# Modulation vectors of a diffusion backbone layer: ada weights as the stationary operand

## The reference, cut to what matters

```python
silu_c = jax.nn.silu(c)              # (1, 1024)
silu_cc = jax.nn.silu(c_ctx)         # (1024,)
sh1, sc1, gt1, sh2, sc2, gt2 = split(silu_c @ ada_w + ada_b, 6)       # ada_w (1024, 6144)
csh1, csc1, cgt1, csh2, csc2, cgt2 = split(silu_cc @ ada_w + ada_b, 6)
hc = modulate(rmsnorm(ctx, norm1_g), csh1, csc1)    # h * (1 + scale) + shift
hx = modulate(rmsnorm(x, norm1_g), sh1, sc1)
...                                  # token mixers (RWKV-7 and mLSTM), merge, gt1
...                                  # second modulation (sh2, sc2), PEER experts, gt2
```

## Time and profile before

| what | value |
|---|---|
| time, median of 3 runs | 3191.59 us (3189.38 to 3191.71) |
| profiled execution: time | 3191.34 us |
| profiled execution: span on the core | 3189.6 us |
| PE, matmul records busy | 2753.4 us (86% of the span) |
| PE, weight loads busy | 2209.1 us (69%) |
| DVE / ACT / POOL busy | 1354.8 / 1006.7 / 701.0 us |
| mean granted TensorE clock | 0.919 of full speed |

### The profile page before, as it was taken

How to read it: one execution, slowest core, us unless ns; L and a number is a source line. 1 busy time by engine, 2 the same in 40 slices (tenths; PEclk the granted TensorE clock), 3 DMA queues, 4 the chain that set the end, 5 groups by cost and what they waited for, 6 DMA issues and landing times. The chain is left out here.

```text
span 3189.6 us, 54953 instructions
## 1 busy us (share of the span) xinstructions
PE 2753.4 (86%) x20248; PEld 2209.1 (69%) x20248; DVE 1354.8 (42%) x2852; ACT 1006.7 (32%) x1666; POOL 701.0 (22%) x540
## 2 busy tenths in 40 slices
PE   5798867657748895996996999999799999999998
PEld 1684144436638883875885788888688888888886
DVE  1221214445566655222899444444001444444443
ACT  2221111141322123223321566666223222222222
POOL 0520000001011202343444555554343000000000
PEclk9899955568979998998998999999899999999999
DMA  4210500000000002222322354544543655555552
GB/s 162 80 58 30 217 0 0 0 7 1 8 1 0 0 5 104 88 86 83 119 88 83 122 207 161 199 176 161 207 148 112 235 190 188 201 190 187 200 192 79
DMA packets 159924, 349.01 MB, mean 109 GB/s; under 512 B 13224, under 2 KB 79272, under 8 KB 156528
## 3 DMA queue, kind: packets, MB, share of 16 engines
q1 hardware_dynamic: 159856, 348.10, 31.4%
HBM read 276.75 MB, written 71.30 MB: 109 GB/s over the span
## 5 line engine op out<-in xcount | busy, mean ns | idle before, releaser
L85 PE MATMUL ps_a<-h_hi,u_hi 128*128 128x512 f32 x1024 | 407.3, 398 | 23.1 <-PEq L105 16.5
L86 PE MATMUL ps_a<-h_hi,u_lo 128*128 128x512 f32 x1024 | 401.0, 392 | 0.0
L87 PE MATMUL ps_a<-h_lo,u_hi 128*128 128x512 f32 x1024 | 400.7, 391 | 0.0
L2360 DVE TENSOR_TENSOR v_lo<-v_raw,v_hi 128x1024 fp32r<-128x1024 f32 x128 | 158.2, 1236 | 564.8 <-ACT v_hi L2318 564.8
L85 PE MATMUL ps_y<-gated_hi,v_hi 128*128 128x512 f32 x768 | 299.5, 390 | 3.1 <-DVE gated_lo L2362 3.1
L86 PE MATMUL ps_y<-gated_hi,v_lo 128*128 128x512 f32 x768 | 299.5, 390 | 0.0
L87 PE MATMUL ps_y<-gated_lo,v_hi 128*128 128x512 f32 x768 | 299.3, 390 | 0.0
L2318 ACT ACTIVATE v_hi<-v_raw 128x1024 fp32r<-128x1024 f32 x128 | 135.8, 1061 | 478.4 <-PE ps_a L87 470.0
L85 PEld LDWEIGHTS ps_a<-h_hi,u_hi 128*128 128x128 f32 x1024 | 194.1, 190 | 62.2 <-issue 22.7
L87 PEld LDWEIGHTS ps_a<-h_lo,u_hi 128*128 128x128 f32 x1024 | 193.6, 189 | 41.0
L86 PEld LDWEIGHTS ps_a<-h_hi,u_lo 128*128 128x128 f32 x1024 | 193.9, 189 | 37.7
(11 more groups left out here) (478 smaller groups left out, 5595.6 us busy)
## 6 DMA issues: line engine op xcount, KB each, us to landing
u_raw<-in_uT SPq DMA_DIRECT2D x128, 512.0 KB, 3.5
v_raw<-in_v SPq DMA_DIRECT2D x128, 512.0 KB, 4.9
a_scratch<-act SPq DMA_DIRECT2D x128, 256.0 KB, 2.2
w_scratch<-w_block SPq DMA_DIRECT2D x8, 4096.0 KB, 12.0
w_ring<-w_scratch SPq DMA_DIRECT2D x64, 512.0 KB, 4.6
gated<-a_scratch SPq DMA_DIRECT2D x128, 256.0 KB, 5.0
ada_ring<-in_ada_w SPq DMA_DIRECT2D x12, 2048.0 KB, 7.9
mg_raw<-in_w_merge SPq DMA_DIRECT2D x36, 512.0 KB, 3.5
```

Of the source, the lines that this page charges most:

```text
L85: pe.matmul(out, wh, xh, start=first, stop=False)
L86: pe.matmul(out, wl, xh, start=False, stop=False)
L87: return pe.matmul(out, wh, xl, start=False, stop=last)
L2360: v.tensor_tensor(vl[:, q], v_raw[:, q], vh[:, q], ALU.subtract).then_inc(v_lo, 1)
```

## The change

The ada weights become the stationary operand and the two conditioning columns the moving one. For each tile, each group of 128 columns and each of the 8 blocks of rows there is one matmul, with 128 x 128 of the ada weights stationary and 128 x 2 of `silu_c` moving; the 8 of a group accumulate in PSUM, in the two columns of `ps_mod` where the turned row stood. `copy_row`, `turn`, the row buffers in SBUF and PSUM and their semaphores go. `add_bias` waits for the last tile's matmuls. The DMAs, the ring of two tiles and its wait stay as they are.

```diff
-    def __init__(self, nc, ctx, a, b, tag, lo, hi, row):
+    def __init__(self, nc, ctx, a, b, tag, lo, hi):
...
-        self.row = row
-        self.ps_row = [ctx.enter_context(nc.psum_tensor(f"ps_row{k}" + tag, [P, MOD_W], F32)) for k in range(2)]
...
     def multiply(self, pe, n):
         pe.wait_ge(self.ring_in[n % 2], (n // 2 + 1) * 16)
-        if n >= 2:
-
-            pe.wait_ge(self.out, n - 1)
-        for k in range(KT):
-            mm = pe.matmul(self.ps_row[n % 2][0:2, :], self.b.silu_c[:, k, :], self.ring[:, n % 2, k, :],
-                           start=(k == 0), stop=(k == KT - 1))
+        for q in range(PER):
+            o = 2 * (n * PER + q)
+            for k in range(KT):
+                mm = pe.matmul(self.ps_mod[:, o:o + 2], self.ring[:, n % 2, k, q * P:(q + 1) * P],
+                               self.b.silu_c[:, k, :], start=(k == 0), stop=(k == KT - 1))
         mm.then_inc(self.mm, 1)
-
-    def copy_row(self, act, n):
-        act.wait_ge(self.mm, n + 1)
-        act.activation(self.row[:, n, :], self.ps_row[n % 2][0:2, :], ACT.Copy).then_inc(self.out, 1)
-
-    def turn(self, pe):
-        pe.wait_ge(self.out, self.hi - self.lo)
-        for n in range(self.hi - self.lo):
-            for q in range(PER):
-                o = 2 * (n * PER + q)
-                mm = pe.matmul(self.ps_mod[:, o:o + 2], self.row[:, n, q * P:(q + 1) * P], self.b.ident[0:2, 0:2],
-                               start=True, stop=True)
-        mm.then_inc(self.turned, 1)
...
-        v.wait_ge(self.turned, 1)
+        v.wait_ge(self.mm, self.hi - self.lo)
```

More of the change, by code:

```diff
@@ L130, in __init__ @@
         self.bias = ctx.enter_context(nc.sbuf_tensor("ada_bias" + tag, [P, N_MOD * KT], F32))
-        self.row = row
-        self.ps_row = [ctx.enter_context(nc.psum_tensor(f"ps_row{k}" + tag, [P, MOD_W], F32)) for k in range(2)]
         self.ps_mod = ctx.enter_context(nc.psum_tensor("ps_mod" + tag, [P, 512], F32))
         self.ring_in = [b.semaphore(nc, f"ada_in{k}" + tag) for k in range(2)]
-        self.bias_in, self.mm, self.out, self.turned, self.done = (
-            b.semaphore(nc, f"mod_{n}" + tag) for n in ("bias_in", "mm", "row_out", "turned", "done"))
+        self.bias_in, self.mm, self.done = (b.semaphore(nc, f"mod_{n}" + tag) for n in ("bias_in", "mm", "done"))
     def load(self, sp, n):
@@ L201, in phase_modulation @@
         dve = sem("mod_dve")
-        mod = Modulation(nc, ctx, a, b, "_1", 0, MOD_FIRST, b.qX[0:2, :, :])
+        mod = Modulation(nc, ctx, a, b, "_1", 0, MOD_FIRST)
         block = ctx.enter_context(nc.Block())
@@ L233, in _ @@
             act.activation(rs[:], rs[:], ACT.Exp, scale=-0.5).then_inc(root_done, 1)
-            for n in range(MOD_FIRST):
-                mod.copy_row(act, n)
             for j in range(KT):
@@ L261, in _ @@
                 mod.multiply(pe, n)
-            mod.turn(pe)
         @block.vector
@@ L1121, in phase_mlstm_gates @@
         rows_done = sem("mlg_rows")
-        mod = Modulation(nc, ctx, a, b, "_2", MOD_FIRST, MOD_TILES, b.acc[0:2, :, :])
+        mod = Modulation(nc, ctx, a, b, "_2", MOD_FIRST, MOD_TILES)
         n_mod = MOD_TILES - MOD_FIRST
@@ L1146, in _ @@
             act.activation(bsum[:], bsum[:], ACT.Ln, bias=1.0).then_inc(act_done, 1)
-            for n in range(2):
-                mod.copy_row(act, n)
             act.wait_ge(want[1], 1)
@@ L1152, in _ @@
             act.activation(rows[:, 4], rows[:, 4], ACT.Exp).then_inc(act_done, 1)
-            for n in range(2, n_mod):
-                mod.copy_row(act, n)
         @block.vector
```

## The result

The changed kernel takes 3288.07 us (median of 4 runs, 3287.61 to 3289.9); the kernel before 3191.32 us (4 runs). The ratio is 1.0305, 95% interval 1.0288 to 1.0323: 3.1% slower, 96.8 us. The profiled execution took 3287.61 us with a span of 3285.6 us. I had forecast 3247 and a range up to 3268: the sign was right and the size too small by 41 us.

The account below looks back on a forecast made before the run. PE's modulation stream was taken to set the end of both phases, at a clock fallen to 0.50. Terms of +18.0 and +38.1 us, +56.1 on 3191.34, gave 3247 us; range 3208 to 3268 for 8 in 10.

Parts of the forecast that it names:

- Which stream sets the end, and that DMAs hide: Both modulation phases: PE's stream sets the end, each microsecond of it counts in the kernel, and all tile DMAs are hidden.
- The clock: Both modulation phases: the new stream lets PE's clock fall at 40.5 us and never raises it from 0.50.
- loads count: Rival, both modulation phases: weight loads of 128 rows hold and raise the clock; -15.1 us, 3176 us; chance 13%.
- the turning's fall at 408.1: Second phase before the change: the clock fell from 1.00 to 0.50 while PE turned, taken as evidence for the new stream.
- The pace: Modulation: a 128-column load with a 2-column matmul takes 0.109 us at 2.4 GHz and 0.2136 us at 1.2 GHz.
- Latency: Rival, modulation: each of 16 matmuls adding to the same PSUM columns may wait for the last; +162 us, 3353; chance 5%.
- the check over 63 steps: Turning in the second phase: 22 steps at one pace and 41 at the other, 11.15 us, agreed with the paces.
- The two terms: Lengthening of the modulation's PE stream: +18.0 us in the first phase and +38.1 us in the second.
- The trust in a page's load rule: Modulation loads: the page's rule gives 107 ns for 128 columns at either clock; the sum used the trace's 214 ns at 1.2 GHz.
- The program's growth: PE's program: 480 more pairs in straight code; fetching could leave gaps, but 64 turning pairs ran without one; no time added.

## Why the prediction was right and wrong

*Which stream sets the end, and that DMAs hide.* Right. DVE's adds follow PE's last pair directly; no tile's DMA but the first of the second phase is waited for.

*The clock.* Right. It fell under loads of 128 rows as under the turning's 2, and the rival "loads count" is out: in the second phase 512 pairs, each half of them without a gap, left it at 0.50. What I had leaned on, the turning's fall at 408.1, carried over.

*The pace.* Right: 0.213 us measured for 0.2136. "Latency" is out. One sum on the way is wrong: (2.42 + 0.18) / 22 is 0.118 and not 0.11. The stretch began with the first pair, so that nothing reaches in over its edge, and 2.42 / 22 = 0.11 is the right reading; the check over 63 steps gives the same, and the 0.109 used carries no error from it.

*The two terms.* 16.6 and 37.4 us, 54.0 together, for 18.0 and 38.1. In the first phase the fast stretch lasted until just before 40, some 5 us, where I allowed 3.9; the transposes took 1.4 us, not 1.9. When the clock falls differs from one execution to the next: with the loop held at slot 40 it fell some 2.4 us into the phase, and the bias add came 52.5 us after PE's start, 19.0 us more than before. PE began the first phase 2.0 us earlier in this execution, and from the first bias add to the second phase's start it took 0.9 us less; that brings the 54.0 to the 51.1 us seen at the next phase. With the loop held in place the whole kernel gave 53.6.

*The trust in a page's load rule.* I had weighed a load at its columns over 1.2 ns (the Trainium skill, "TensorE: Matmul & The Clock Gate", section LDWEIGHTS) against the trace, and had gone by the trace. The measurement keeps to that: 0.213 us a pair at the lower level.

*The program's growth.* Here the prediction failed. It said: "PE's program grows by 768 - 288 = 480 pairs in straight code; fetching it could leave gaps, but 64 pairs of turning ran without one". I asked whether the new code could be fetched in time, and it could. I did not ask what the new code moves. It pushed a loop that starts some 500 us behind the second phase from 7 blocks of instruction memory to 8, and at each of its six returns the loop then fetched its own body again: 47.1 us by the traces, 52 us with the old modulation at that slot. In the sum this term was zero. The next phase itself lost nothing, as the prediction said (4.67 us from the bias add to its first matmul, 4.68 before); what was false is the silent step that nothing further on would move.

The Trainium skill, "Runtime: NRT & Kernel Launch", section Instruction fetch mechanics, gives TensorE 128 KiB of instruction memory, refilled in 16 KiB blocks of 256 instructions, and says that a taken branch to a target outside the current window of two pages waits for a fetch. The packets of 16 KB agree with the block's size. The window of two does not agree: the loop touches 7 blocks at slot 64, its branch goes back over more than two of them, and the passes have no instruction packet. That 8 blocks are fetched again in each pass is in the traces; why 8 are too many, when by the page's 128 KiB 8 would fit, no run here shows.

## What to carry to other kernels

Before making the long operand stationary and a few columns moving, look at what happens to the granted clock in a stretch of the trace that does just that: here the pace of a load and its matmul, and not the columns that it moves, was the cost, and it doubled with the low clock (0.109 to 0.213 us). A cheap step that seems in the way (turning rows) can be moved off the path instead of removed, but only as much of it comes free as the engine had waited. And when an edit changes how many instructions an engine has, compare the instruction queue's packets and the length of one pass of every large loop behind it before explaining the total: a loop at the edge of what stays resident can cost as much as the edit.

## What was not expected of the hardware

A loop of 1721 TensorE instructions (by the count) took 33.3 us a pass when it began at slot 40 or 64 of a block, 41 us at slot 224 after the change and 39 to 44 us there with the old modulation; at slot 80, with 9 instructions over the edge, only two of six passes in the profiled execution were long, and the runs spread from 3191.98 to 3215.36 us. Each long pass brought 9 instruction packets, in all three kernels that had them. With 64 moving columns under each load, the clock stayed at 1.00 where it was entered at 1.00 and at 0.50 where it was entered at 0.50. With 128, a modulation that multiplies 64 times as much made the kernel 69 us faster.
